# Moving the splitting of squares and keys from ScalarE and VectorE to GpSimd in the second attention, with the norm one unit later

## The chip, the cores and the metric

The kernel runs on one core of a Trainium2 chip. The metric is the device time of one execution in microseconds (us), as the median of several runs. A core has five engines with instruction queues of their own: TensorE (PE, matmuls; PEld its weight loads), VectorE (DVE), ScalarE (ACT), GpSimd (POOL) and SyncE (SP, which here only issues transfers). Each engine works its list in order and waits on semaphores for the others.

## The reference

Three blocks follow one another on 1024 tokens of width 1024, all in float32: a layer with sliding-window attention and pooling, a layer with a long convolution, and a second block with 16 meta tokens in front (1040 tokens), of which this is the part that matters:

```
y_attn = forgetting_attention(q, k, v, log_f)        # 8 heads of 64, causal, softmax with a decay
y_conv = b_gate * causal_depthwise_conv(c_gate * u, conv_w)
y = concat(head_rms_norm(y_attn, 8, g), head_rms_norm(y_conv, 8, g))
h = h + y @ w_out                                    # then norm, a feed-forward of width 4096, norm
```

`head_rms_norm` divides each head's 64 values of a token by the root of the mean of their squares.

## The kernel before

Values are kept transposed: 128 channels (two heads, a "pair") on the partitions and tokens along the row. A float32 product is made from parts: a value is rounded to a "high" part in TensorE's format (fp32r) and the "low" part is value minus high; the product is then made with both. Rounding is a copy with an output of that type, the low part a subtraction.

The second attention is a list of 80 units (`NU`), 20 for each of four pairs (pair 0 to 3), 10 for each head. A unit is one step over 128 keys, or over three short rests of keys together, for one half of 512 queries. A head has 3 units for its first half and 7 for its second, so that of the 20 units of a pair numbers 2, 9, 12 and 19 end a half (`half_end(m)`, m = 0 to 15 over the whole attention). I call unit 13 of a pair "unit 13", and so on; units count from 0.

In each unit n TensorE does in order: the scores of unit n+2, a "max tile" for the next pair where `MAXES` has one (units 8 to 15 and 17 to 24, where 20 to 24 are units 0 to 4 of the next pair; 8 tiles for each of its heads), a "turn" of the finished maxima where `TURNS` has one (unit 16, and unit 5 of the next pair), the values of unit n (line 1654), and the "head product" of a finished half (lines 1667 and 1668: the sum over a head's channels of its squares, high part and low part, into bank 4). ScalarE does the exponential of each unit (line 2318), the squares `SQ` of a half (2326), their high part `SH` (2331), the keys' high part `KH` of the next pair (2299, in unit 3), the queries' high part `QH` (2304, in unit 4), and the square root of the sums in unit 6 (2335), for which the function table is changed and changed back. VectorE copies the output of a half to `Q` (3082), makes `SL`, the low part of the squares (3087), `KL` and `QL` (3032, 3036), copies the head product's result to `K` (3095, function `norms`), takes the maxima of each max tile (3046; lines 3049 and 3050 end them), the reciprocals (3101), the scaled heads (3106) and their low part `YL` (3111). `CVL` (3115) is the same for the convolution.

What ties them: a max tile waits until VectorE has taken the tile before it (one bank pair is used by all). The first max tile of a pair (unit 8) waits until `extended(c)` on SyncE has brought six transfers of that pair's `KH`, `QH` and decay rows to `KE` and `QE`. SyncE issues them once the high parts of keys and queries are there. All orders are written out by hand; nothing is scheduled by a planner.

GpSimd brings the weights' high parts (`high(p)`: a transfer, line 964) and makes their low parts (`low(p)`, line 973). When the attention starts it also writes the zeros and ones of `KE`, `QE` and `QM` (`init_extended`, `init_slot`), then issues one more weight load with its low part, and has nothing more until the output product after the attention. TensorE's max tile is line 1585 (with its mask 1588), the scores are 1632, 1633 and 1637, the turn is 1600.

## Time and profile before

| | |
|---|---|
| median of 3 runs | 2019.5 us (2018.78 to 2023.27) |
| the profiled execution's own time | 2022.04 us |
| its span in the profile | 2020.2 us |
| mean granted TensorE clock | 0.988 of full speed |
| PE busy / DVE / ACT / POOL, share of the span | 96% / 64% / 36% / 56% |
| the second attention, first scores to first output product | 1105.78 to 1277.84 us of the span |

Times in the rows are us from the start of the span. In a row of the timeline the first number is the start, the second the duration, and the bracket at its end says how long the engine sat idle before it and who ended that. The granted clock is a share of full speed: 1.00 is 2.4 GHz, and 0.50 would be 1.2 GHz throughout.

### The profile page before, as it was taken

The page shows a single profiled execution, that of the slowest core. Times are in us where ns is not written, and L with a number is a line of the kernel's source. Part 1 is how long each engine was busy: PE and PEld are TensorE (multiplying, and loading weights), DVE is VectorE, ACT ScalarE, POOL GpSimd, SP SyncE. Part 2 cuts the span into 40 slices and gives each one's busy share as a digit, 9 for nine tenths or more (in the row PEclk, how much of TensorE's full clock was granted, in tenths as well). Part 3 has the DMA queues.
Part 4 walks back from the last instruction along what each step waited for, and adds up shares of the span by engine and source line. Part 5 has one row for each costly group of instructions (what it writes and reads, how often), then busy time and mean ns, then how long its engine had stood idle before and what let it go on. Part 6 is the DMA issues. An engine that isn't in the chain of part 4 may idle for free.

```text
span 2020.2 us, 25037 instructions
## 1 busy us (share of the span) xinstructions
PE 1946.2 (96%) x9228; PEld 1563.9 (77%) x9228; DVE 1298.9 (64%) x1856; ACT 729.1 (36%) x1221; POOL 1135.9 (56%) x936
## 2 busy tenths in 40 slices
PE   8999999999999999999999989999999999999997
PEld 7787877788777788778887555687788887888886
DVE  5127663679998997251764676467544447777778
ACT  4002653342246443230211554324322324545542
POOL 3221115469989995535442100127777778888884
PEclk8999999999999999999999999999999999999998
DMA  5432117556555554538425442345656768675652
GB/s 193 143 120 72 43 43 250 171 177 188 177 167 176 171 174 148 186 133 257 152 85 133 106 90 53 146 152 161 219 198 224 234 200 299 220 267 206 213 193 99
DMA packets 104504, 335.43 MB, mean 166 GB/s; under 512 B 12672, under 2 KB 12928, under 8 KB 103616
## 3 DMA queue, kind: packets, MB, share of 16 engines
q1 hardware_dynamic: 55616, 192.74, 29.7%
q0 software_dynamic: 30384, 106.44, 15.5%
q10 hardware_dynamic: 18384, 34.66, 4.7%
q8 instruction: 74, 1.21, 0.2%
q14 instruction: 46, 0.38, 0.1%
HBM read 272.75 MB, written 46.20 MB: 158 GB/s over the span
## 4 chain that ended last, share of the span: by engine, by line
issue 33%; POOL 31%; PE 30%; DVE 3%; DMA 2%; ACT 1%; POOLq 0%; SPq 0%; DVEq 0%; ACTq 0%
PE PS L1256 15%; PE PS L1789 13%; POOL WL L973 12%; POOL VSL L1192 3%; POOL RBM L1036 3%; POOL WL L1187 2%; POOL SQH L1036 2%; POOL WH L964 2%; DMA WH<-weights 1%; POOL VS L1184 1%; POOL VS L1179 1%; POOL VS L1176 1%; POOL WL L1194 1%; POOL WH L1162 1%; DVE ACC L3330 1%
## 5 line engine op out<-in xcount | busy, mean ns | idle before, releaser
L1256 PE MATMUL PS<-XHM,WH 128*128 128x512 f32 (+2 forms) x1464 | 525.3, 381 | 18.3 <-POOL WL L973 7.9
L1256 PE MATMUL PS<-XLM,WH 128*128 128x512 f32 (+2 forms) x1464 | 513.0, 373 | 0.0
L1256 PE MATMUL PS<-XHM,WL 128*128 128x512 f32 (+2 forms) x1464 | 512.4, 372 | 0.0
L964 POOL DMA_DIRECT2D WH<-weights x149 | 84.7, 568 | 694.9 <-PE PS L1256 680.0
L973 POOL TENSOR_TENSOR WL<-WRAW,WH 128x1024 fp32r<-128x1024 f32 x149 | 361.1, 2424 | 28.8 <-DMA WH<-weights 20.3
L1256 PEld LDWEIGHTS PS<-XHM,WH 128*128 128x128 f32 x1464 | 270.7, 189 | 80.0 <-issue 15.7
L1256 PEld LDWEIGHTS PS<-XLM,WH 128*128 128x128 f32 x1464 | 277.0, 189 | 49.2 <-issue 1.7
L1256 PEld LDWEIGHTS PS<-XHM,WL 128*128 128x128 f32 x1464 | 276.8, 189 | 48.3
L2770 DVE SCALAR_TENSOR_TENSOR PS<-G,TAPW,PS 128x512 f32<-128x512 f32 x319 | 215.6, 746 | 0.6
L3330 DVE TENSOR_TENSOR ACC<-ACC,PS 128x1024 f32<-128x1024 f32 (+1 forms) x113 | 119.8, 1073 | 16.1 <-PE PS L1256 13.2
L1256 PE MATMUL PS<-OPH,VSH 128*128 128x512 f32 x256 | 99.9, 390 | 2.9 <-issue 2.7
L1256 PE MATMUL PS<-OPH,VSL 128*128 128x512 f32 x256 | 99.6, 389 | 0.0
L1256 PE MATMUL PS<-OPL,VSH 128*128 128x512 f32 x256 | 99.6, 389 | 0.0
L3310 DVE TENSOR_TENSOR OPL<-PS,OPH 128x512 fp32r<-128x512 f32 x98 | 67.5, 689 | 45.6 <-ACT PS L2458 44.5
L2062 ACT ACTIVATE YG<-G,TAPW 128x512 f32<-128x512 f32 x120 | 80.4, 717 | 38.1 <-POOL RBM L1036 31.1
L1654 PE MATMUL PS<-PT,VX 128*128 128x512 f32 (+4 forms) x224 | 85.7, 485 | 6.8 <-ACT PT L2318 6.8
L1192 POOL TENSOR_TENSOR VSL<-VS,VSH 128x512 fp32r<-128x512 f32 x64 | 83.3, 1322 | 5.1 <-ACT VSH L2465 5.1
L2535 DVE TENSOR_TENSOR PS<-PS,SQH 128x512 f32<-128x512 f32 x60 | 41.5, 694 | 61.6 <-ACT SQH L1926 61.1
L1256 PE MATMUL PS<-OPH,WH 128*128 128x512 f32 x192 | 74.9, 390 | 2.3 <-DVE OPL L3306 1.7
L2458 ACT COPY PS<-OPR 128x512 f32<-128x512 f32 x98 | 57.4, 585 | 53.7 <-DVE OPL L3310 53.7
L1036 POOL TENSOR_TENSOR RBM<-RBM,YG 128x512 f32<-128x512 f32 x58 | 74.8, 1290 | 2.8 <-ACT YG L2062 2.8
L2465 ACT ACTIVATE VSH<-VS 128x512 fp32r<-128x512 f32 x64 | 40.1, 632 | 98.1 <-POOL VS L1179 57.9
(383 smaller groups left out, 3979.9 us busy)
## 6 DMA issues: line engine op xcount, KB each, us to landing
WRAW<-weights SPq DMA_DIRECT2D x211, 512.0 KB, 3.5
WH<-weights POOLq DMA_DIRECT2D x195, 512.0 KB, 4.5
OPR<-inner SPq DMA_DIRECT2D x56, 512.0 KB, 6.4
inner<-STAGE ACTq DMA_DIRECT2D x56, 256.0 KB, 4.1
inner<-TOUT ACTq DMA_DIRECT2D x48, 256.0 KB, 4.3
XTOK<-x SPq DMA_DIRECT2D x8, 512.0 KB, 9.6
x_kept<-X SPq DMA_DIRECT2D x4, 1024.0 KB, 8.2
X<-x_kept SPq DMA_DIRECT2D x8, 512.0 KB, 5.5
```

Of the source, the lines that this page charges most:

```text
L964: g.dma_start(WH[:, u, :], weights[WORDER[p]]).then_inc(w_hi[u], 16)
L973: g.tensor_tensor(WL[:, u, :], WRAW[:, u, :], WH[:, u, :].bitcast(F32), ALU.subtract)\
L1036: g.tensor_tensor(tap_acc(q), tap_acc(q), tap_buffer(h, i, q), ALU.add).then_inc(tap_sum[q], 1)
L1192: g.tensor_tensor(VSL[e][:, two], VS[e][:, two], VSH[e][:, two].bitcast(F32), ALU.subtract).then_inc(w_ready, 1)
L1256: m = nc.tensor.matmul(dst[:, a:b], w, v[:, a:b], start=first and n == 0, stop=last and n == 2)
L1654: m = nc.tensor.matmul(o[:, q0 - half * HALF:q0 - half * HALF + w], VX[0:keys, j, c, HD * e:HD * e + P], PT2[n % 3][0:keys, a:a + w], star ...
L1789: m = nc.tensor.matmul(dst, a[:, c], b[:, k, :], start=new and k == 0 and i == 0, stop=k == 3 and i == 2, skip_group_check=True)
L2062: nc.scalar.activation(tap_buffer(h, i, q), col, ACT.Copy, scale=tap).then_inc(tap_product, 1)
L2458: nc.scalar.copy(bank(LOW_BANK), OPR[x][:, a, :]).then_inc(a_hi, 1)
L2770: ins = v.scalar_tensor_tensor(out=src if last else bank(b), in0=src, scalar=weight, in1=bank(was), op0=ALU.mult, op1=ALU.add)
L3310: v.tensor_tensor(OPL[x][:, a, :], bank(LOW_BANK), OPH[x][:, a, :].bitcast(F32), ALU.subtract).then_inc(a_split, 1)
L3330: v.tensor_tensor(dst, dst, src, ALU.add).then_inc(evacuated, 1)
```

## The change

GpSimd takes over 15 of 16 pairs of `SH` and `SL` (`squares_split(m)`; the last stays on ScalarE and VectorE) and the three `KH` of pairs 1 to 3. It does the first `SH`, `SL` and `KH` right behind the constants of `KE` and `QE`, ahead of its last weight load, and the others behind that. TensorE's head product comes 3 units after the end of a half instead of 2, and VectorE's copy of its result (`norms`) 4 instead of 3. Semaphores are renamed and counted apart for keys and queries (`k_hi`; `q2_taken`, which also counts four earlier steps). ScalarE's `queries_hi` now waits itself for the transfers that read the old parts.

```diff
@@ SyncE, extended(c)
-                sp.wait_ge(kq_hi, 2 * c + 2)
+                sp.wait_ge(k_hi, c + 1)
+                sp.wait_ge(q2_taken, 4 + c + 1)
@@ GpSimd
+            def keys_hi(c):
+                pool.wait_ge(ext_in[(c - 1) % 2], 96 * ((c - 1) // 2 + 1))
+                for e in range(2):
+                    pool.wait_ge(slot_in[e], 80 * c)
+                g.tensor_copy(KH2[:], K2[:, c, :]).then_inc(k_hi, 1)
+
+            def squares_split(m):
+                pool.wait_ge(o2_sq, m + 1)
+                g.tensor_copy(SH2[m % 2][:], SQ2[m % 2][:]).then_inc(o2_hi, 1)
+                pool.wait_ge(o2_hi, m + 1)
+                g.tensor_tensor(SL2[m % 2][:], SQ2[m % 2][:], SH2[m % 2][:].bitcast(F32), ALU.subtract).then_inc(o2_lo, 1)
+
                     init_extended(1)
                     initialized(4)
+                    squares_split(0)
+                    keys_hi(1)
+                if p == P_OUT2 + 2:
+                    for m in range(1, 2 * HEADS - 1):
+                        if m % 4 == 0 and m // 4 + 1 < PAIRS:
+                            keys_hi(m // 4 + 1)
+                        squares_split(m)
@@ TensorE
-                    if n - 2 in ended:
-                        head_norm(ended[n - 2])
+                    if n - 3 in ended:
+                        head_norm(ended[n - 3])
@@ ScalarE
-                if n - 1 in ended:
-                    squares_hi(ended[n - 1])
                 c, s = divmod(n, 2 * PER_HEAD)
-                if s == 3 and c + 1 < PAIRS:
-                    keys_hi(c + 1)
@@ VectorE
                 if n in ended:
                     output2(ended[n])
-                if n - 1 in ended:
-                    squares_lo(ended[n - 1])
-                if n - 2 in ended:
-                    norms(ended[n - 2])
+                if n - 3 in ended:
+                    norms(ended[n - 3])
```

GpSimd's list at the start of the attention, from the last constant (`SMALL` is only a mark) on. Before:

```order
L1026 MEMSET SMALL 128x1
L964 DMA WH<-weights 128x1024
L973 TENSOR_TENSOR WL<-WRAW,WH 128x1024
L964 DMA WH<-weights 128x1024
L973 TENSOR_TENSOR WL<-WRAW,WH 128x1024
```

and with the change:

```order
L1027 MEMSET SMALL 128x1
L1109 CAST SH_0_125<-SQ_0_118 128x512
L1111 TENSOR_TENSOR SL_0_123<-SQ_0_118,SH_0_125 128x512
L1105 CAST KH_99<-K_89 128x1040
L965 DMA WH<-weights 128x1024
L974 TENSOR_TENSOR WL<-WRAW,WH 128x1024
L1109 CAST SH_1_126<-SQ_1_119 128x512
L1111 TENSOR_TENSOR SL_1_124<-SQ_1_119,SH_1_126 128x512
```

The weight load and its subtraction, the first thing behind the constants before, stand behind two roundings and a subtraction.

VectorE's list in units 10 to 14 of pair 1. Before:

```order
L3082 COPY Q_91<-PS 64x512
L3101 RECIPROCAL K_89<-K_89 128x256
L3046 TENSOR_REDUCE SMALL<-PS 128x1
L3087 TENSOR_TENSOR SL_1_124<-SQ_1_119,SH_1_126 128x512
L3106 SCALAR_TENSOR_TENSOR Q_91<-Q_91,GAINS,K_89 128x1024
L3046 TENSOR_REDUCE SMALL<-PS 128x1
L3095 COPY K_89<-PS 64x512
L3046 TENSOR_REDUCE SMALL<-PS 128x1
L3082 COPY Q_91<-PS 64x512
L3111 TENSOR_TENSOR YL<-Q_91,YH 128x1024
L3046 TENSOR_REDUCE SMALL<-PS 128x1
```

and with the change:

```order
L3094 COPY Q_91<-PS 64x512
L3113 RECIPROCAL K_89<-K_89 128x256
L3058 TENSOR_REDUCE SMALL<-PS 128x1
L3118 SCALAR_TENSOR_TENSOR Q_91<-Q_91,GAINS,K_89 128x1024
L3058 TENSOR_REDUCE SMALL<-PS 128x1 x2
L3094 COPY Q_91<-PS 64x512
L3107 COPY K_89<-PS 64x512
L3123 TENSOR_TENSOR YL<-Q_91,YH 128x1024
L3058 TENSOR_REDUCE SMALL<-PS 128x1 x3
```

`SL` is gone, and the copy to `K` has moved from ahead of the maxima of unit 12 to between the copy to `Q` and `YL` of unit 13.

## Rows read from the trace of the kernel before

**Rows 1.** The page, its first line.
```profile
span 2020.2 us, 25037 instructions
```

**Rows 2.** Windows: the attention; busy us and (instructions) by engine, clock, DMA share, GB/s.
```profile
1105.78:1277.84 172.06, 153.05 (x709) 96.14 (x710) 113.83 (x152) 85.83 (x143) 10.64 (x13) 0.98 0.37 81
```

**Rows 3.** Timeline of PE: stops, first max tile, one turn.
```profile
1118.30 0.71 PE L1667 MATMUL PS<-SH,HN 128*128 128x512 f32 x1 [1.86 <-DVE SL L3087]
...
1125.61 0.31 PE L1585 MATMUL PS<-KE,QE 128*128 128x144 f32 x1
...
1160.27 0.27 PE L1600 MATMUL PS<-IDENT,SMALL 128*8 128x128 f32 x1
...
1165.65 1.56 PE L1654 MATMUL PS<-PT,VX 128*128 128x512 f32 x2 [2.05 <-ACT PT L2318]
...
1175.37 0.50 PE L1585 MATMUL PS<-KE,QE 128*128 128x512 f32 x1 [0.80 <-DVE SMALL L3046]
...
1183.07 0.68 PE L1585 MATMUL PS<-KE,QE 128*128 128x512 f32 x2 [1.41 <-DVE SMALL L3046]
...
1188.03 0.27 PE L1600 MATMUL PS<-IDENT,SMALL 128*8 128x128 f32 x1 [0.36 <-DVE SMALL L3050]
...
1263.17 0.50 PE L1667 MATMUL PS<-SH,HN 128*128 128x512 f32 x1 [0.56 <-DVE SL L3087]
...
1269.10 0.50 PE L1667 MATMUL PS<-SH,HN 128*128 128x512 f32 x1 [0.67 <-DVE SL L3087]
```

**Rows 4.** Windows: behind the first stop; pair 1 and pair 2, unit 7 to unit 11.
```profile
1118.30:1122.12 3.82, 3.82 (x8) 2.17 (x9) 3.74 (x4) 2.82 (x4) 0.00 (x0) 0.55 0.99 213
...
1165.65:1175.37 9.72, 8.92 (x38) 5.58 (x38) 6.70 (x9) 3.38 (x7) 0.00 (x0) 0.82 0.65 138
1211.39:1219.52 8.13, 7.33 (x37) 4.61 (x37) 6.70 (x9) 3.38 (x7) 0.00 (x0) 1.00 0.78 163
```

**Rows 5.** GpSimd: two roundings' nearest kin, a subtraction of 512, the weights' subtraction.
```profile
L985 POOL CAST IDENTB<-IDENT 128x128 bf16<-128x128 f32 x1 | 0.3, 289 | 0.1
L1010 POOL TENSOR_SCALAR_AFFINE_SELECT QE<-QE 64x1024 fp32r<-64x1024 f32 x4 | 4.1, 1036 | 0.6 <-POOL QE L1009 0.2
L1192 POOL TENSOR_TENSOR VSL<-VS,VSH 128x512 fp32r<-128x512 f32 x64 | 83.3, 1322 | 5.1 <-ACT VSH L2465 5.1
...
1115.32 2.36 POOL L973 TENSOR_TENSOR WL<-WRAW,WH 128x1024 fp32r<-128x1024 f32 x1
```

**Rows 6.** Timeline of VectorE, start of the attention.
```profile
1115.81 2.44 DVE L3087 TENSOR_TENSOR SL<-SQ,SH 128x512 fp32r<-128x512 f32 x1 [1.34 <-ACT SH L2331]
1118.17 1.23 DVE L3032 TENSOR_TENSOR KL<-K,KH 128x1040 fp32r<-128x1040 f32 x1
...
1121.21 3.48 DVE L3115 TENSOR_TENSOR CVL<-G,CVH 128x1024 fp32r<-128x1024 f32 x3
```

**Rows 7.** SyncE's queue, first of the six transfers for pair 1; the window of them.
```profile
1116.82 0.53 SPq L746 DMA_DIRECT2D KE<-KH  x1
...
1116.25:1123.12 6.87, 5.01 (x14) 2.69 (x13) 6.79 (x6) 5.42 (x9) 1.43 (x1) 0.75 0.93 225
```

**Rows 8.** Timeline of VectorE: maxima of unit 4, then units 12 and 13 of pair 1.
```profile
1158.56 1.22 DVE L3046 TENSOR_REDUCE SMALL<-PS 128x1 f32<-128x1024 f32 x1
...
1177.64 0.67 DVE L3095 COPY K<-PS 64x512 f32<-64x512 f32 x1
...
1180.06 0.69 DVE L3082 COPY Q<-PS 64x512 f32<-64x512 f32 x1 [0.76 <-ACT SQ L2326]
1180.78 1.23 DVE L3111 TENSOR_TENSOR YL<-Q,YH 128x1024 fp32r<-128x1024 f32 x1
1182.04 0.97 DVE L3046 TENSOR_REDUCE SMALL<-PS 128x1 f32<-128x784 f32 x1
```

**Rows 9.** ScalarE: the squares, and the roundings that leave it, grouped by form.
```profile
L2326 ACT ACTIVATE SQ<-PS,HSCALE 128x512 f32<-128x512 f32 x16 | 11.0, 687 | 28.8 <-PE PS L1654 28.8
...
L2331 ACT ACTIVATE SH<-SQ 128x512 fp32r<-128x512 f32 x16 | 10.1, 630 | 0.0
```

More of the change, by code:

```diff
@@ L473, in build @@
         ext_init = sem("ext_init")
-        kq_hi = sem("kq_hi")
+        k_hi = sem("k_hi")
         kq_lo = sem("kq_lo")
@@ L498, in build @@
         hn_inv = sem("hn_inv")
-        yc_sq = sem("yc_sq")
+        q2_taken = sem("q2_taken")
         yc_sum = sem("yc_sum")
@@ L1686, in attention2 @@
                     values(n)
-                    if n - 2 in ended:
-                        head_norm(ended[n - 2])
+                    if n - 3 in ended:
+                        head_norm(ended[n - 3])
             def heads_conv(c):
-                pe.wait_ge(yc_sq, c + 1)
+                pe.wait_ge(q2_taken, c + 1)
                 if c >= 1:
@@ L2255, in _ @@
                 wait_freed(act, (IN2, I_B + c, 1))
-                nc.scalar.activation(Q2[:, c, :], CU[:, c, META:], ACT.Square).then_inc(yc_sq, 1)
+                nc.scalar.activation(Q2[:, c, :], CU[:, c, META:], ACT.Square).then_inc(q2_taken, 1)
             def value_taken(n):
@@ L2290, in _, with keys_hi, queries_hi @@
                 value_taken(n)
-            def keys_hi(c):
-                if c >= 1:
+            def keys_hi():
+                wait_freed(act, (IN2, 20, 1))
+                nc.scalar.activation(KH2[:], K2[:, 0, :], ACT.Copy).then_inc(k_hi, 1)
+            def queries_hi(c):
+                if c == 0:
+                    act.wait_ge(evacuated, USE[C_IN2 + I_Q] + 1)
+                else:
                     act.wait_ge(ext_in[(c - 1) % 2], 96 * ((c - 1) // 2 + 1))
@@ L2296, in keys_hi @@
                         act.wait_ge(slot_in[e], 80 * c)
-                else:
-                    wait_freed(act, (IN2, 20, 1))
-                nc.scalar.activation(KH2[:], K2[:, c, :], ACT.Copy).then_inc(kq_hi, 1)
-            def queries_hi(c):
-                if c == 0:
-                    act.wait_ge(evacuated, USE[C_IN2 + I_Q] + 1)
-                nc.scalar.activation(QH2[:], Q2[:, c, :], ACT.Copy).then_inc(kq_hi, 1)
+                nc.scalar.activation(QH2[:], Q2[:, c, :], ACT.Copy).then_inc(q2_taken, 1)
             def max_hi(h):
@@ L2343, in conv_hi @@
                 nc.scalar.activation(CVH[:, c, :], CU[:, c, META:], ACT.Copy).then_inc(cv_hi, 1)
-            keys_hi(0)
+            keys_hi()
             queries_hi(0)
@@ L2372, in _ @@
                     max_hi(TURNS[n])
-            for m in range(2 * HEADS - 1):
-                if half_end(m) + 2 >= NU:
-                    squares_hi(m)
             squares(2 * HEADS - 1)
@@ L3030, in keys_lo @@
             def keys_lo(c):
-                dve.wait_ge(kq_hi, 2 * c + 1)
+                dve.wait_ge(k_hi, c + 1)
                 v.tensor_tensor(KL2[:, c, :], K2[:, c, :], KH2[:].bitcast(F32), ALU.subtract).then_inc(kq_lo, 1)
             def queries_lo(c):
-                dve.wait_ge(kq_hi, 2 * c + 2)
+                dve.wait_ge(q2_taken, 4 + c + 1)
                 v.tensor_tensor(QL2[:, c, :], Q2[:, c, :], QH2[:].bitcast(F32), ALU.subtract).then_inc(kq_lo, 1)
@@ L3143, in _ @@
             output2(2 * HEADS - 1)
+            squares_lo(2 * HEADS - 1)
             for m in range(2 * HEADS):
-                if half_end(m) + 2 >= NU:
-                    squares_lo(m)
-            for m in range(2 * HEADS):
-                if half_end(m) + 3 >= NU:
+                if half_end(m) + 4 >= NU:
                     norms(m)
```

## Prediction, before the changed kernel was run

> **What bounds the kernel now.** I read the page first: a span of 2020.2 us [rows 1], against 2022.04 us for that execution's own time and 2019.5 us for the median, so 1.8 us lie around the span and the profiled execution was 2.5 us slower than the median. I add what I find to the median. The change touches only the second attention. Its window [rows 2] shows PE busy 153 of 172 us, DVE 114, ACT 86, POOL 11. So TensorE bounds the stretch, ScalarE has half its time free, and taking work off it is worth nothing by itself. What can be won is the 19 us in which TensorE stands, plus what a low clock costs. Then I read the timeline of PE for its stops [rows 3]. The reader is to see four kinds:
>
> - 1.86 us on `SL` at the start; then 0.56 and 0.67 us on `SL` in pair 3, where no max tiles fill the time. Sum 3.1 us. These are what the change is made of.
> - 2.05 us behind the square root, when ScalarE changes tables (three times, in unit 7 of pairs 1 to 3).
> - 0.80 and 1.41 us at the max tiles of units 11 and 14, on VectorE's maxima (twice each, pairs 1 and 2).
> - 0.36 us at the turn of unit 16 (three times, pairs 0 to 2), on VectorE again.
>
> The windows [rows 4] add the clock: 0.55 in the 3.82 us behind the first stop, 0.82 behind the 2.05 us stop of pair 1, 1.00 behind the same stop of pair 2. The same work took 9.72 and 8.13 us, so one drop to 1.2 GHz costs 1.6 us.
>
> **Prices on GpSimd.** A rounding of 128x512 isn't in the trace. The cast of 128 elements takes 0.289 us, a one-input operation of 1024 takes 1.036 [rows 5]: 0.83 ns an element and 0.18 fixed, thus 0.61 us for 512 and 1.05 for 1040. The upper bound is a two-input subtraction of that size, 1.32 us (and 2.4 for 1040). I take the lower, since the cast is the same instruction. A split is then 0.61 + 1.32 + 0.15 between them = 2.1 us (at most 2.8) from the squares on. TensorE asks for it three units later, each 172/80 = 2.15 us on average, so in the steady part no head product waits for `SL`. The Trainium skill, "GPSIMD Engine Reference", section 4.1, has one-input work "roughly line-rate"; the two rows agree with that.
>
> **The start of the attention.** Before, `SL` took 2.44 us instead of 0.68 beside the weights' subtraction (1115.32 to 1117.68); it ended 0.57 behind it [rows 5, 6]. A VectorE instruction with two SBUF inputs stands still while GpSimd reads. Now `SL` is on GpSimd itself: GpSimd is free at 1114.7, so `SH` 0.61, `SL` 1.32, `KH` 1.05 and gaps give `SL` at about 1116.8 and `KH` at 1118.0. TensorE, which was done with unit 4 at 1118.30 - 1.86 = 1116.4, finds its `SL` one unit later without a wait. Its way from there to the first max tile was 1125.61 - 1118.30 = 7.3 us, of which 1.6 were the clock. It could be there at 1116.4 + 5.7 = 1122.1, 3.5 us earlier than before. Two things stand in front of that.
>
> First, the six transfers for that max tile. SyncE issued the first at 1116.82 when `QH` was there; now it waits for `KH`, 1118.0. The weight load of 512 KB was issued 2 us ahead of them, and now falls among them, at 1118.0 to 1118.6. At 225 GB/s the window of 6.87 us moved 1.55 MB, which is the load and the six (0.52 + 1.04 MB) [rows 7]. Both together begin now some 1.5 us behind their issue, about 1119.3, and are over at 1126.1 if they share evenly, at 1124.5 if the load ends last. I take 1125.7: the max tile comes when it came before.
>
> Second, VectorE. `KL` began at 1118.17 and begins at 1118.05 now. Behind it come `QL` (1.2), the copy to `K` (0.68) and three `CVL` (3.48) [rows 6, 8], over at 1124.7 before. The weights' subtraction (2.36) now falls on this row of two-input instructions: `QL` or a `CVL` stands still for it, and the row ends at 1127.0. The maxima of unit 8 end at 1127.5, and the second max tile waits 0.5 us or so for them.
>
> So TensorE stands for 3.5 us ahead of unit 8, at the place of the 1.86 us, and with that the clock should fall as it did there, for 1.6 us. **Term: +1.5 us** (bounds: -1.0, transfers by 1124.5 and no drop; +3.0, roundings at the upper bound).
>
> The rule that speaks against this change stands in the Trainium skill, "SBUF — State Buffer", section "Who interferes with whom": a VectorE instruction with two SBUF inputs and a GpSimd instruction that reads SBUF exclude each other for a whole instruction. By that rule, the trace agrees: 2.44 against 0.68 us.
>
> **Units 12 to 14 of pairs 1 and 2.** The stop of 1.41 us is a chain from the end of unit 12's values: squares on ScalarE 0.69 [rows 9], copy to `Q` 0.69, `YL` 1.23, maxima 0.97 [rows 8], max tile. The copy to `K` (0.67) now stands in this chain, between `Q` and `YL`. And GpSimd wakes on the same squares: `SH` for 0.61, then `SL` from 0.9 to 2.2 us behind them, while `YL` wants to start 1.4 us behind them. `YL` stands still till 2.2, 0.8 us. Against that the chain begins 0.6 us earlier: the head product went from unit 11 to behind the values of unit 12 (two matmuls of 512 columns at 2.4 GHz, 0.21 us each, some 0.47 with the gaps), and the removed `SL` (0.67) lets VectorE follow. -0.6 + 0.67 + 0.8 = +0.9; gaps between queues are less in the longer chain, I take **+0.6 each, +1.2**. Bounds: -0.4 in all if `YL` gets in first (with a rounding of 1.3 us it does), +1.8 if the subtraction is slower beside it.
>
> **The turn of unit 16**, three times 0.36 us: the head product now stands between the last max tile and the turn, and fills that stop. **-1.1.** The 0.80 us stop of unit 11 hangs on the squares, the copy to `Q` and a reciprocal, of which none moves: 0.
>
> **Units 2 to 5.** The copy to `K` also comes into the chain from the end of unit 2 through squares, `Q` and the maxima of unit 3 to the max tile of unit 4, which TensorE meets without a stop today, I take it just so: 0.67 less the 0.47 us of the moved head product is 0.2, three times, and the same once in unit 13 of pair 0: **+0.8**. The turn in unit 5 follows the maxima of unit 4: they end at 1159.78, the two small closing operations follow, the turn is at 1160.27 [rows 3, 8]. So the chain VectorE, turn, ScalarE, table change, values is what gives the 2.05 us stop its end. Moving the head product from ahead of the turn to behind it shortens the stop and not the time: 0.
>
> **Pair 3.** 0.56 + 0.67 = **-1.2**, as `SL` is there. `YL` may be late behind GpSimd, but no max tile waits.
>
> **ScalarE** loses 15 x 0.63 us [rows 9] and three roundings of keys. It waits for TensorE most of the time, so 0.
>
> Sum: +1.5 + 1.2 - 1.1 + 0.8 - 1.2 = **+1.2 us**, 2020.7 us. What 3 runs of this kernel can tell from no change is about 0.2%, 4 us. So I forecast no measurable change.
>
> **The rivals.**
>
> *The start is won (faster).* If the transfers land by 1122 and the weights' subtraction meets VectorE's copy from PSUM rather than `QL` and `CVL`, TensorE runs through: -3.5 with the clock kept, and `YL` in front of GpSimd (-0.4). -3.5 - 0.4 - 1.1 + 0.8 - 1.2 = -5.4, 2014.1 us. For it: the 1.86 us stop and its clock drop are real, and `SL` no longer suffers. Against it: 1.55 MB at 225 GB/s, started 1.2 us later, can't be there by 1122. Chance 0.2.
>
> *The clock falls more often (slower).* The new stops of 2.2 us at unit 14 (1.41 and 0.6 more, with 0.2 of the moved head product) are as long as the one that cost 1.6 us in pair 1. If both, and one more of the three behind the square root, are followed by 1.2 GHz: 3 x 1.6 = 4.8, +6.0 in all, 2025.5 us. It decides from two more drops on (+4.4). For it: a drop behind 1.86, and one of three behind 2.05. Against it: two of three had none. Chance 0.2.
>
> *The change does what it says, and it is worth only that.* If neither GpSimd nor the copy to `K` costs anything, and the start stays tied to its transfers: 0 - 1.1 - 1.2 = -2.3, 2017.2 us. This lies within 0.2% as well and shares the 0.6 with the forecast (0.2 of it).
>
> **How the numbers follow.** Forecast 0.4, the third rival 0.2, the two others 0.2 each. Faster by over 0.2% (under 2015.5): 0.2; slower (over 2023.5): 0.2; within: 0.6. The bounds of the terms, taken together, are -1.0 - 0.4 - 1.1 + 0.8 - 1.2 = -2.9, and -1.6 more if the drop in pair 1 doesn't come, and +3.0 + 1.8 - 1.1 + 0.8 - 0.6 = +3.9 without more drops. The range 2015.0 to 2025.0 takes them in, and leaves out the faster rival's figure and the far end of the slower one.
>
> **What would show it.** Right: no stop on `SL` anywhere but at the last half; a stop of 3 us or more ahead of the first max tile of pair 1, ended by a transfer, and a low clock behind it; one of VectorE's two-input instructions near 1119 to 1125 lasting over 3 us; `YL` of pairs 1 and 2 lasting 2 us; the stop of unit 14 at about 2 us; no stop at unit 16; the rounding of 512 near 0.6 us. Wrong: the first max tile at 1122 to 1124, `YL` at 1.23 us, or roundings of 1.3 us and more, with `SL` late for its head product.

## The result, and the profile after

The changed kernel takes 2024.57 us (median of 22 runs, 2020.53 to 2034.54), the kernel before 2019.57 us beside it (22 runs, 2013.6 to 2024.89). The ratio is 1.0027, 95% interval 1.0019 to 1.0035: slower by 5.0 to 5.5 us. I had forecast 2020.7 us and no change that can be told. The profiled execution took 2026.82 us, with a span of 2025.0; the first line of the page, to be held against [rows 1]:

```profile
span 2025.0 us, 25042 instructions
```

The windows of the attention (columns as in [rows 2]): the whole of it, its start up to the first max tile of pair 1, from there to the turn of unit 16, and the stretch from the turn of unit 5 to that of unit 16 in pair 1 and in pair 2.

```profile
1106.94:1282.41 175.47, 152.78 (x710) 96.89 (x710) 107.66 (x137) 75.47 (x125) 42.00 (x46) 0.97 0.37 79
1106.94:1128.60 21.66, 14.17 (x64) 8.92 (x65) 12.70 (x12) 12.44 (x19) 13.49 (x16) 0.95 0.78 181
1128.60:1147.13 18.53, 18.24 (x78) 11.96 (x79) 9.80 (x16) 4.43 (x8) 3.77 (x4) 0.88 0.20 46
1165.50:1193.22 27.72, 23.39 (x102) 14.16 (x102) 20.85 (x25) 11.76 (x18) 3.78 (x4) 0.94 0.32 69
1211.59:1237.69 26.10, 21.74 (x103) 13.57 (x104) 20.85 (x25) 11.76 (x18) 3.78 (x4) 1.00 0.35 73
```

And the two windows of the kernel before that answer to the second and the third of them:

```profile
1105.78:1125.61 19.83, 16.13 (x64) 9.51 (x65) 12.38 (x13) 13.70 (x20) 10.64 (x13) 0.91 0.74 176
1125.61:1142.25 16.64, 16.13 (x80) 10.49 (x80) 11.67 (x18) 5.99 (x11) 0.00 (x0) 1.00 0.38 78
```

The reader is to see: the attention is 3.41 us longer (175.47 for 172.06). The start alone is 1.83 us longer, and the stretch behind it 1.89, in which TensorE runs the same matmuls (but for one head product) at a clock of 0.88 for 1.00. Of pairs 1 and 2 the same list takes 27.72 and 26.10 us, once with a stretch of low clock and once without: 1.62 us for a stretch, as in [rows 4]. In pair 1 the stretch has moved. Before, it lay behind the stop at the square root [rows 4]; now the clock is 1.00 from there to the max tile of unit 14, and the 3.3 us at 1.2 GHz lie right behind that tile's stop:

```profile
1170.89:1187.09 16.20, 13.45 (x65) 8.65 (x65) 13.22 (x15) 6.74 (x12) 3.78 (x4) 1.00 0.37 78
1187.09:1193.22 6.13, 6.13 (x18) 3.08 (x18) 2.68 (x5) 0.00 (x0) 0.00 (x0) 0.72 0.00 0
```

The stops of TensorE (timeline of PE, to be held against [rows 3]):

```profile
1128.60 0.49 PE L1605 MATMUL PS<-KE,QE 128*128 128x144 f32 x1 [6.06 <-DMA KE<-cum_rows]
...
1162.98 0.73 PE L1605 MATMUL PS<-KE,QE 128*128 128x512 f32 x2 [0.47 <-DVE SMALL L3058]
1165.50 0.27 PE L1620 MATMUL PS<-IDENT,SMALL 128*8 128x128 f32 x1 [0.27 <-DVE SMALL L3062]
1170.89 1.12 PE L1674 MATMUL PS<-PT,VX 128*128 128x512 f32 x2 [1.58 <-ACT PT L2337]
...
1187.09 0.68 PE L1605 MATMUL PS<-KE,QE 128*128 128x512 f32 x2 [1.96 <-DVE SMALL L3058]
```

No stop on `SL` is left in the attention, and none at the turn of unit 16. In their place stand 6.06 us ahead of the first max tile, on a transfer; 0.47 us at the max tile of unit 4; and 1.96 us at unit 14, where it was 1.41.

VectorE and GpSimd at the start (timelines; [rows 6] and the last of [rows 5] before), and SyncE's first and last transfer for the max tile ([rows 7]):

```profile
1116.24 1.28 POOL L1111 TENSOR_TENSOR SL<-SQ,SH 128x512 fp32r<-128x512 f32 x1
...
1117.48 1.04 POOL L1105 CAST KH<-K 128x1040 fp32r<-128x1040 f32 x1
...
1118.47 0.57 POOL L965 DMA_DIRECT2D WH<-weights  x1
...
1118.56 4.00 DVE L3044 TENSOR_TENSOR KL<-K,KH 128x1040 fp32r<-128x1040 f32 x1 [2.93 <-POOL KH L1105]
...
1118.68 0.54 SPq L747 DMA_DIRECT2D KE<-KH  x1
...
1119.07 2.38 POOL L974 TENSOR_TENSOR WL<-WRAW,WH 128x1024 fp32r<-128x1024 f32 x1
...
1122.54 0.59 SPq L749 DMA_DIRECT2D KE<-cum_rows  x1
```

`KL` takes 4.00 us for 1.23: the weights' subtraction has the memory from 1119.07 to 1121.45, and `KL` ends 1.1 us behind it at 1122.56. `KH` ends at 1118.52 and the first transfer is issued 0.16 us later, 11.74 us behind the first scores for 11.04 before.

Unit 13 of pair 1, timeline of VectorE and GpSimd ([rows 8] before):

```profile
1183.07 0.69 DVE L3094 COPY Q<-PS 64x512 f32<-64x512 f32 x1 [0.77 <-ACT SQ L2345]
...
1183.10 0.61 POOL L1109 CAST SH<-SQ 128x512 fp32r<-128x512 f32 x1 [4.95 <-ACT SQ L2345]
...
1183.79 0.68 DVE L3107 COPY K<-PS 64x512 f32<-64x512 f32 x1
...
1183.79 1.28 POOL L1111 TENSOR_TENSOR SL<-SQ,SH 128x512 fp32r<-128x512 f32 x1
...
1184.40 1.75 DVE L3123 TENSOR_TENSOR YL<-Q,YH 128x1024 fp32r<-128x1024 f32 x1
```

and GpSimd's groups by form, whose mean in ns is the number ahead of the last bar:

```profile
L1105 POOL CAST KH<-K 128x1040 fp32r<-128x1040 f32 x3 | 3.1, 1048 | 2.2 <-DMA QM<-QL 2.2
L1109 POOL CAST SH<-SQ 128x512 fp32r<-128x512 f32 x15 | 9.2, 610 | 120.7 <-ACT SQ L2345 120.6
L1111 POOL TENSOR_TENSOR SL<-SQ,SH 128x512 fp32r<-128x512 f32 x15 | 19.2, 1277 | 1.2
```

`YL` takes 1.75 us for 1.23 and ends at 1186.15, 1.1 us behind GpSimd's `SL` (1185.07).

### The profile page after: what moved, and what is told of

The parts are those of the page before. It is cut to its first block, busy times and chain, and to the rows that moved or that the text cites. A ratio compares the mean times of both kernels' runs of the same rounds, so it can differ in the third digit from the quotient of the medians.

```text
span 2025.0 us, 25042 instructions
## 1 busy us (share of the span) xinstructions
PE 1948.0 (96%) x9228; PEld 1565.6 (77%) x9228; DVE 1292.4 (64%) x1841; ACT 718.6 (35%) x1203; POOL 1166.8 (58%) x969
## 3 DMA queue, kind: packets, MB, share of 16 engines
q8 instruction: 74, 1.21, 0.2%
## 4 chain that ended last, share of the span: by engine, by line
PE 34%; POOL 31%; issue 27%; DVE 4%; DMA 2%; ACT 2%; SPq 0%; POOLq 0%; DVEq 0%; ACTq 0%
PE PS L1276 15%; PE PS L1809 13%; POOL WL L974 13%; POOL VSL L1212 3%; POOL RBM L1037 3%; PE PS L1674 2%; POOL WL L1207 2%; POOL SQH L1037 2%; POOL WH L965 2%; DMA WH<-weights 1%; POOL VS L1204 1%; POOL VS L1199 1%; PE PS L1605 1%; POOL VS L1196 1%; POOL WL L1214 1%
## 5 line engine op out<-in xcount | busy, mean ns | idle before, releaser
L3318 DVE TENSOR_TENSOR OPL<-PS,OPH 128x512 fp32r<-128x512 f32 x98 | 67.6, 690 | 45.4 <-ACT PS L2470 44.5
L2082 ACT ACTIVATE YG<-G,TAPW 128x512 f32<-128x512 f32 x120 | 80.4, 717 | 38.1 <-POOL RBM L1037 31.2
L1109 POOL CAST SH<-SQ 128x512 fp32r<-128x512 f32 x15 | 9.2, 610 | 120.7 <-ACT SQ L2345 120.6
```

What stands on the lines that cost most here:

```text
L2082: nc.scalar.activation(tap_buffer(h, i, q), col, ACT.Copy, scale=tap).then_inc(tap_product, 1)
L3318: v.tensor_tensor(OPL[x][:, a, :], bank(LOW_BANK), OPH[x][:, a, :].bitcast(F32), ALU.subtract).then_inc(a_split, 1)
```

## How the experiments are read

The table gives every kernel that ran. "To tile" is the time from the first scores to the first max tile of pair 1, "to turn" from there to the turn of unit 16 of pair 0, "att." the whole attention, all in us, from one profiled execution each. "Low" is the time at 1.2 GHz in the attention, worked out as 2 x (1 - granted clock) x length, summed over its eight sections between turns. The ratio is of timed runs against the kernel before.

| kernel | to tile | to turn | att. | low | median | ratio (95% interval) |
|---|---|---|---|---|---|---|
| before | 19.83 | 16.64 | 172.06 | 6.9 | 2019.57 | |
| before, second look | 21.26 | 16.64 | 171.91 | 6.8 | | |
| after | 21.66 | 18.53 | 175.47 | 9.9 | 2024.57 | 1.0027 (1.0019 to 1.0035) |
| after, second look | 21.38 | 18.66 | 175.25 | 9.9 | | |
| e1_defer | 19.22 | 21.12 | 182.06 | 27.6 | 2025.87 | 1.0021 (1.0009 to 1.0034) |
| e2_keys | 20.34 | 22.30 | 184.35 | 31.2 | 2023.84 | 1.0025 (1.0009 to 1.0041) |
| e6_hold | 21.66 | 18.42 | 175.31 | 10.3 | 2025.74 | 1.0022 (1.0009 to 1.0034) |
| e8_kcopy | 21.76 | 17.85 | 174.85 | 16.8 | 2022.11 | 1.0011 (1.0000 to 1.0021) |
| e10_ylfirst | 21.82 | 21.05 | 177.96 | 17.1 | 2022.72 | 1.0016 (1.0004 to 1.0028) |
| e5_sooner | 21.55 | 18.79 | 175.40 | 10.0 | 2022.81 | 1.0023 (1.0011 to 1.0034) |
| e4_later | 19.94 | 16.32 | 172.08 | 6.9 | 2017.93 | 0.9984 (0.9971 to 0.9996) |
| e9_best | 19.98 | 17.28 | 172.49 | 6.9 | 2019.39 | 0.9994 (0.9983 to 1.0005) |
| e12_fill | 21.45 | 16.31 | 171.38 | 0 | 2017.51 | 0.9984 (0.9971 to 0.9997) |
| e15_fill8 | 21.53 | 16.31 | 171.62 | 0 | 2023.41 | 1.0009 (0.9998 to 1.0021) |
| e16_fill14 | 21.58 | 18.47 | 173.68 | 6.6 | 2019.40 | 1.0001 (0.9985 to 1.0018) |
| e13_fillb | 18.35 | 16.62 | 172.06 | 6.8 | 2018.74 | 0.9990 (0.9980 to 0.9999) |
| e14_laterfill | 18.48 | 16.32 | 169.07 | 0 | 2019.45 | 0.9996 (0.9985 to 1.0006) |

One caution holds for all of it. Outside the attention these kernels run the same instructions, and yet the first scores stand at 1100.0 us in one profile and at 1108.0 in another, and what follows the attention takes 740.5 to 746.1 us. A single profile says where time goes in the attention, to a few tenths; it doesn't say within 3 us what the median will be.

## Experiments on the start

**e1_defer** does the second `SH` and `SL` ahead of the last weight load, so that this and its subtraction come later.

```diff
                     squares_split(0)
                     keys_hi(1)
+                    squares_split(1)
...
-                    for m in range(1, 2 * HEADS - 1):
+                    for m in range(2, 2 * HEADS - 1):
```

> The changed kernel with its last weight load and that load's subtraction moved on GpSimd from behind the first split and the keys to behind the second split, 13 us later. Theory 1 (the loss is made at the start: late transfers for the first max tile of pair 1, the weight load among them, and the low clock behind the stop): KL takes 1.24 us instead of 4.00, the stop ahead of the first max tile falls from 6.06 us to 3 or 4, the attention (first scores to first output product) from 175.5 us to 172 to 173.5. Theory 2 (the loss is made in units 3 and 13, by the copy to K in the chain and by YL standing behind GpSimd): the stop may shrink, but the attention stays at 175 to 176 us and the time at 1.002 to 1.003 of before.

The max tile comes 2.4 us sooner (19.22) and `KL` runs alone (timeline of VectorE):

```profile
1117.79 1.24 DVE L3045 TENSOR_TENSOR KL<-K,KH 128x1040 fp32r<-128x1040 f32 x1 [2.94 <-POOL KH L1105]
1118.95 1.22 DVE L3049 TENSOR_TENSOR QL<-Q,QH 128x1024 fp32r<-128x1024 f32 x1
```

So the weight load holds the transfers up and its subtraction holds `KL` up. But nothing was won, neither in the timed runs (1.0021) nor in the attention, which both theories had put at 176 us or less and which took 182.06: the windows behind the max tile and of pair 1 show the clock at 0.76 and 0.88, 10.1 and 7.0 us of low clock (and 7.0 again in pair 2).

```profile
1125.38:1146.50 21.12, 20.83 (x79) 13.47 (x79) 9.80 (x16) 4.47 (x8) 6.66 (x6) 0.76 0.33 76
1164.87:1194.21 29.34, 24.99 (x102) 15.15 (x102) 21.00 (x25) 11.75 (x18) 3.78 (x4) 0.88 0.31 65
```

**e6_hold** has SyncE issue the next transfers (those of pair 1's scores) only when the six have landed.

```diff
             for c in range(1, PAIRS):
+                if c == 1:
+                    sp.wait_ge(ext_in[1], 96)
                 slots(2 * c)
```

> The changed kernel with one wait more on SyncE: the five transfers of slots(2) are issued only when the six for the first max tile of pair 1 have landed. In the changed kernel they were issued 1.2 us behind the last of the six, since TensorE had been early. Theory 1a (they share the bandwidth with the last of the six): the stop falls from 6.06 us to about 3.9, the first max tile comes 2.2 us earlier, the attention is 173 to 173.5 us. Theory 1b (the six are slow by themselves, with the weight load): the stop stays at 6 us.

The stop is 6.06 us again. The traffic that follows the six costs them nothing. This kernel also shows what my forecast of the landing left out, since nothing else runs behind the six. Windows of 1 us, first transfer issued at 1112.84, max tile released at 1122.75:

```profile
1113.09:1114.09 1.00, 1.00 (x6) 0.51 (x4) 1.00 (x1) 1.00 (x3) 0.98 (x2) 1.00 0.34 41
...
1115.09:1116.09 1.00, 1.00 (x5) 0.52 (x5) 1.00 (x1) 1.00 (x3) 0.52 (x1) 1.00 1.09 291
...
1120.09:1121.09 1.00, 0.00 (x0) 0.00 (x0) 1.00 (x2) 0.00 (x0) 0.00 (x0) 0.61 0.64 132
1121.09:1122.09 1.00, 0.00 (x0) 0.00 (x0) 0.76 (x1) 0.00 (x0) 0.00 (x0) 0.50 0.09 25
```

The last two columns are the DMA share and GB/s. The bulk of the bytes flows from about 1113.7 to about 1120.8; the windows add up to some 1.6 MB, which in that time are some 225 GB/s, as I had reckoned. But the flow doesn't end at its full rate. Windows of a quarter of a microsecond:

```profile
1120.00:1120.25 0.25, 0.00 (x0) 0.00 (x0) 0.25 (x1) 0.00 (x0) 0.00 (x0) 1.00 1.04 214
1120.25:1120.50 0.25, 0.00 (x0) 0.00 (x0) 0.25 (x1) 0.00 (x0) 0.00 (x0) 0.63 0.75 148
...
1120.75:1121.00 0.25, 0.00 (x0) 0.00 (x0) 0.25 (x1) 0.00 (x0) 0.00 (x0) 0.50 0.38 82
...
1121.50:1121.75 0.25, 0.00 (x0) 0.00 (x0) 0.25 (x1) 0.00 (x0) 0.00 (x0) 0.50 0.05 16
1121.75:1122.00 0.25, 0.00 (x0) 0.00 (x0) 0.10 (x1) 0.00 (x0) 0.00 (x0) 0.50 0.00 0
```

From 1120.25 on the rate falls, the last bytes come before 1121.75, and TensorE is released at 1122.75. So it is released some 2 us behind the end that bytes and rate would give: about 1 us in which the flow thins out, and 1.0 us between the last bytes and the release. The column ahead of the last two says when the clock fell: between 1120.25 and 1120.50, while TensorE (0.00 busy) had been standing for some 3.6 us.

**e2_keys** leaves the key rounding of pair 1 on ScalarE, in unit 3 as before; GpSimd does only the squares there.

```diff
                     squares_split(0)
-                    keys_hi(1)
...
+                if n == 3:
+                    keys_hi(1)
```

> The changed kernel with the high part of the keys of pair 1 alone back on ScalarE in unit 3, as before the change; the splits and the two other roundings of keys stay on GpSimd. Theory 1: the six transfers begin 1 us or more earlier, the stop ahead of the first max tile is 3 to 4.5 us instead of 6.06, the attention 172.5 to 174 us. Theory 2: 175 to 176 us.

The stop is 4.11 us and the max tile at 20.34, 1.3 us sooner; the clock is low for 12.9 us behind it, and the attention is far longer than either theory said (184.35 us). The time is that of the changed kernel. The key rounding's place is worth 1.3 us of the 3.1 us by which the tile is late, and the weight load 2.4; they overlap.

## Experiments on units 12 to 14 and on the later norm

**e10_ylfirst** lets GpSimd wait with `SL` until `YL` is written, for the halves that meet.

```diff
                 pool.wait_ge(o2_hi, m + 1)
+                if m % 4 == 2 and m >= 4:
+                    pool.wait_ge(y2_split, m // 4)
                 g.tensor_tensor(SL2[m % 2][:], SQ2[m % 2][:], SH2[m % 2][:].bitcast(F32), ALU.subtract).then_inc(o2_lo, 1)
```

> The changed kernel with one wait more on GpSimd: in pairs 1 to 3 the subtraction SL of the half that ends in unit 12 comes behind YL. Theory (YL stands behind that subtraction): YL takes 1.23 us instead of 1.75, the stop of unit 14 falls from 1.96 to 1.45 us, nothing else moves, attention 1.0 us shorter at the same clock. Rival (YL is slow for another cause): 1.75 us again.

Timelines of VectorE and GpSimd in pair 1 of this kernel:

```profile
1183.36 1.21 DVE L3125 TENSOR_TENSOR YL<-Q,YH 128x1024 fp32r<-128x1024 f32 x1
...
1184.71 1.26 POOL L1113 TENSOR_TENSOR SL<-SQ,SH 128x512 fp32r<-128x512 f32 x1 [2.04 <-DVE YL L3125]
```

`YL` takes 1.21 us for 1.75, and the stop of unit 14 is 1.41 for 1.96: GpSimd's `SL` was 0.55 us of that stop. The section from the turn of unit 5 to that of unit 16 gets 0.55 us shorter (25.55 us for 26.10). The attention as a whole didn't get 1.0 us shorter, as forecast for an equal clock, but 2.5 longer (177.96 us): 17.1 us of low clock for 9.9, of which 10.1 lie behind the first max tile (0.76 in 21.05 us), where this edit changes nothing. `SL` also comes late now for a head product of pair 3, a stop of 0.60 us.

**e8_kcopy** puts VectorE's copy to `K` behind the maxima of its unit.

```diff
-                if n - 3 in ended:
-                    norms(ended[n - 3])
...
                 if n in MAXES:
                     max_part(*MAXES[n])
+                if n - 3 in ended:
+                    norms(ended[n - 3])
```

> The changed kernel with VectorE's copy to K put behind the maxima of its unit instead of ahead of them (and so behind YL in unit 13). The copy's 0.67 us leave the chain to the max tile of unit 14 and of unit 4: the stop of 1.96 us falls to 1.3 to 1.6 (YL then begins 0.7 us sooner and meets GpSimd's subtraction for longer, it lasts 2.3 us or gets in first), the stops of 0.47 us in unit 4 go, with a clean clock one pair takes 44.0 us instead of 44.5. If fewer drops of the clock follow the shorter stop, the time is at 1.000 to 1.002 of before; if the start alone decides, 1.002 to 1.003.

The stop of unit 14 falls to 0.93 us, that of unit 4 is gone, and the section from the turn of unit 16 to that of unit 5 takes 17.70 us for 18.37. The copy to `K` in the two chains costs 1.0 us at unit 14 and 0.67 at unit 4, a pair. Ratio 1.0011; the gain of some 4 us in all that these make is partly eaten, as the attention has 16.8 us of low clock for 9.9.

**e4_later** is the kernel before with the head product and the copy to `K` one unit later, and nothing else.

```diff
-                    if n - 2 in ended:
-                        head_norm(ended[n - 2])
+                    if n - 3 in ended:
+                        head_norm(ended[n - 3])
...
-                if n - 2 in ended:
-                    norms(ended[n - 2])
+                if n - 3 in ended:
+                    norms(ended[n - 3])
```

> The kernel before with only the last part of the change: head product and copy to K one unit later, all roundings and subtractions where they were. Theory 1 (GpSimd's part is what costs): the 1.86 us stop on SL and the low clock behind it go, the first max tile of pair 1 comes some 2 us earlier, the stops of 0.56 and 0.67 us in pair 3 go, YL takes 1.23 us: attention 168 to 170.5 us against 172.1, time 0.998 to 0.999 of before. Theory 2 (the later norm costs, by the copy to K in units 3 and 13): attention 172 us or more, time 1.000 to 1.002.

**e5_sooner** is the other half, the changed kernel with `n - 3` put back to `n - 2` in both places.

> The changed kernel with the head product and the copy to K where they were before (two and three units behind the end of a half), the splits on GpSimd. The head product of a half then asks for SL one unit sooner. If GpSimd's splits alone cost the time and the later norm is the part that wins: the first stop on SL is short (SL at 11.6 us behind the first scores, about when TensorE comes for it), the max tile of unit 8 still at 21.6 us, no copy to K in the chain of unit 14 (stop there 1.2 to 1.6 us in place of 1.96), turn of unit 16 with a stop of 0.3 again; ratio 1.002 to 1.005. If the copy to K in that chain is the cost: attention shorter than 175.5 by 1 us or more, ratio about 1.000.

The two halves give 0.9984 and 1.0023. What loses is GpSimd's part of the change: in e5 TensorE stands for 5.06 us ahead of the first max tile, which comes at 21.55 us. In e5 the stops of units 14 and 16 are those of before (1.41 and 0.36 us), and still the attention takes 175.40 us: the cost isn't in that chain. The later norm costs nothing: by its profile it leaves the attention as long as it was (172.08), and the interval of its ratio ends just under 1. The attention of 168 to 170.5 us that I had expected of e4 didn't come. The stop on `SL` is gone, but a stop of 1.61 us on the transfers stands ahead of the first max tile, and there are two stretches of low clock again, the first now some 3 us behind the first scores (clock 0.51 and 0.50 from 1102.97 to 1104.97).

**e9_best** is e4_later with the copy to `K` behind the maxima, and the last weight load behind the second squares.

```diff
                     initialized(4)
+                    pool.wait_ge(o2_sq, 2)
```

> The kernel before with the later head product and the copy to K behind the maxima, and with the last weight load and its subtraction on GpSimd held till the second squares (13 us later); nothing is moved to GpSimd. From what the single parts gave: SL at the start takes 0.68 us, the six transfers have the bandwidth for themselves, the first max tile comes at 17.5 to 19 us from the first scores instead of 19.8, no or a short low clock behind, pairs 1 and 2 take 43.9 to 44.2 us each at full clock, pair 3 0.8 us less. Attention 166 to 169 us, time 0.996 to 0.998 of before.

Its max tile comes at 19.98 us behind a stop of 1.65 on the transfers (e4_later: 19.94 and 1.61), a max tile behind it waits 1.05 us for VectorE, and so does the turn of unit 5, 0.87 us. The expectation (attention 166 to 169 us, ratio 0.996 to 0.998) failed: 172.49 us and 0.9994. Nothing is won over e4_later.

## Experiments on the clock

Here idle matmuls of 512 columns, whose result nobody reads, stand where TensorE would stand still. They are ahead of the wait, and one takes 0.24 us (the 25 of e12_fill 5.94).

**e12_fill**: 25 ahead of the first max tile of pair 1, 7 ahead of the max tile of unit 14 in pairs 1 and 2.

```diff
...
+                if h == 2 and i == 0:
+                    for _ in range(25):
+                        nc.tensor.matmul(bank(6), KE[0][0][:, 0:P], QE[0][0][:, 0:HALF], start=True, stop=True)
                 if i == 0:
                     pe.wait_ge(ext_in[r], 96 * (h // 4 + 1))
```

> The changed kernel with matmuls that compute nothing used, put where TensorE would stand: 25 of 512 columns ahead of the wait for the six transfers (6.06 us before), 7 ahead of the wait of unit 14 in pairs 1 and 2 (1.96 us). They go to banks that are written anew afterwards. No other instruction moves. Theory C (the clock behind the stops makes most of the loss, and its varying length is why single runs differ): the max tiles come at the same places within 0.3 us, no 1.2 GHz behind unit 8, the attention is 171 to 173 us against 175.5, the time at 0.999 to 1.001 of before. Rival (the clock is only a companion, chains of VectorE and transfers set the time behind the stops as well): attention 174.5 us or more, time 1.002 or more.

**e15_fill8** has only the 25, **e16_fill14** only the 7.

> The changed kernel with idle matmuls only in its 6 us stop ahead of the first max tile of pair 1, not ahead of unit 14. If the 6 us stop alone makes the clock fall: clock 1.00 in pair 0, and pairs 1 and 2 without the low stretch that stood there too, attention 172 or less, ratio 0.998 to 0.9995. If the stops of 1.96 us at unit 14 make it fall as well: a stretch of 1.6 us is left in one or two of pairs 1 and 2, attention 173 to 175, ratio 1.000 to 1.002.

> The changed kernel with idle matmuls only ahead of the max tile of unit 14 of pairs 1 and 2, its 6 us stop ahead of the first max tile left as it is. Filled at the start alone it ran at a ratio of 1.0009, filled at both at 0.9984, unfilled at 1.0027. If the two places cost the clock each by itself: ratio 1.0005 to 1.0015, low clock of about 6 us around and behind the first max tile, none in pairs 1 and 2 or one stretch. If the start is the cause and unit 14 only follows: ratio 1.002 to 1.003.

**e13_fillb** is the control: the kernel before, with 7 ahead of its first head product and 5 ahead of the max tile of unit 14. **e14_laterfill** is e4_later with 6 ahead of the first max tile and 5 at unit 14.

> The kernel before, with idle matmuls of 512 columns whose result nobody reads: 7 ahead of the first head product (they fill its stop of 1.86 us) and 5 ahead of the max tile of unit 14 of pairs 1 and 2 (they fill most of 1.41 us). It is the control for the run that filled the stops of the changed kernel. Theory A (low clock behind stops costs the kernel before little, the changed kernel much): the low clock behind the first stop goes, 1.6 us, so the attention takes 170 to 170.5 us, and the ratio to the kernel before is 0.998 to 1.000. Theory B (the filling gains 0.4% in any kernel, whatever the splits do): ratio 0.995 to 0.997 and less scatter of single runs.

> The kernel before with the head product and the copy to K one unit later alone, and idle matmuls in its stops: 6 ahead of the first max tile of pair 1 (stop 1.61 us), 5 ahead of the max tile of unit 14 (1.42 us). If the gain of the later norm and the cost of the clock are separate: the attention at 172.1 less one or two stretches of 1.6 us, 169 to 170.5, ratio 0.996 to 0.998, under both. If the gain of the later norm was only a kept clock, as the filled changed kernel's was, nothing is left to fill and the ratio stays at 0.998 to 0.999.

Windows of the attention of e12_fill, e15_fill8, e16_fill14 and e13_fillb, a row each:

```profile
1101.22:1272.60 171.38, 157.93 (x748) 102.02 (x749) 107.55 (x137) 75.43 (x125) 42.03 (x46) 1.00 0.37 81
```

```profile
1102.59:1274.21 171.62, 154.65 (x735) 99.37 (x735) 107.58 (x137) 75.42 (x125) 42.03 (x46) 1.00 0.37 81
```

```profile
1102.54:1276.22 173.68, 154.26 (x723) 98.88 (x724) 107.10 (x137) 75.42 (x125) 42.63 (x46) 0.98 0.37 80
```

```profile
1103.95:1276.01 172.06, 156.93 (x727) 99.32 (x727) 113.94 (x152) 85.72 (x143) 10.66 (x13) 0.98 0.38 81
```

The reader is to see the column ahead of the last two, the clock. In e12 the first max tile comes when it came in the changed kernel (at 21.45 us), TensorE does more, and the attention is 4.1 us shorter, with the clock at 1.00. In the timed runs that is 0.43% (1.0027 to 0.9984). Each place alone gives a part: 1.0001 with unit 14 filled, 1.0009 with the start filled. The same treatment of the kernel before gives 0.10%. Between the kernels filled in this way, e12 and e13, nothing is left that the timed runs can tell (0.9984 and 0.9990). The idle matmuls make no wait end sooner, so what they give back is the clock's. Several forecasts failed all the same: e13 kept 6.8 us of low clock in the attention (in pairs 1 and 3) and took 172.06 us, not 170 to 170.5; e14 had none and took 169.07 us, as forecast, but its ratio of 0.9996 is under neither theory; and e16's 1.0001 lies below the range of both of its theories.

The mean granted clock of every timed run is also on record, to 0.001. The same formula turns it into time at 1.2 GHz over the whole execution:

| kernel | timed runs | mean clock | low, us | mean span, us |
|---|---|---|---|---|
| before (beside the experiments) | 122 | 0.9887 | 45.4 | 2018.9 |
| after | 22 | 0.9872 | 51.9 | 2023.5 |
| e1_defer | 12 | 0.9867 | 53.6 | 2023.7 |
| e4_later | 12 | 0.9902 | 39.7 | 2016.0 |
| e12_fill | 11 | 0.9910 | 36.3 | 2016.2 |
| e15_fill8 | 12 | 0.9882 | 47.8 | 2021.0 |

The means of low time of the changed kernels are good to some 2 us. The 122 runs were not made beside the 22, and the runs that were have no clock on record; this may shift the difference by a microsecond. A stretch of 3.3 us cost 1.6, so I count half of it as lost. This estimate splits the changed kernel's 4.6 us (2023.5 less 2018.9) into 3.2 of clock and 1.4 of waits. It gives e12 4.6 us of clock back, beside 1.9 us more of waits, and it says why e15 is slower than e12 though its profiled attention is as short: it has 11.5 us more of low clock. Its profile shows where that can lie: a granted clock of 0.988 with none of it in the attention is some 48 us at 1.2 GHz outside. So for the timed runs most of the loss is the clock. That it is the clock behind the longer stops is shown only in so far as filling them took it away.

What isn't shown is the share of each stop. The stretch of low clock in pair 1 went away when the start was filled (e15: 26.17 us for 27.72), and also when unit 14 was (e16: 26.09). In e15 the stops of unit 14 were 2.05 us long and the clock was 1.00 behind them; in both looks at the changed kernel it fell behind the one of pair 1.

**Second looks.** The changed kernel and the one before once more, unchanged, for a profile alone.

> A second look at the changed kernel. If the stretches of low clock in the attention belong to the kernel: again 6 to 7 us of low clock around the first max tile of pair 1 and one stretch of 3.3 us in pair 1 or 2, attention 174 to 177 us. If they belong to the execution: any sum from 0 to 20 us of low clock, attention 171.5 to 182; in both cases the same stops on the same releasers to within 0.1 us.

> A second look at the kernel before. If the stretches belong to the kernel: 3.6 us of low clock behind the stop on SL at the start, one stretch of 3.3 us in pair 1, attention 171.5 to 172.5. If they belong to the execution: 3.6 us at the start and none to three stretches elsewhere, attention 170.3 to 175.

Windows from the first scores to the first max tile of pair 1 and on to the turn of unit 16, changed kernel:

```profile
1107.19:1128.57 21.38, 14.17 (x64) 8.91 (x65) 12.70 (x12) 12.43 (x19) 13.49 (x16) 0.96 0.78 182
1128.57:1147.23 18.66, 18.39 (x78) 12.00 (x79) 9.80 (x16) 4.43 (x8) 3.77 (x4) 0.87 0.21 47
```

and the first of the two in the kernel before:

```profile
1102.85:1124.11 21.26, 17.55 (x64) 10.13 (x65) 12.43 (x13) 13.67 (x20) 10.65 (x13) 0.84 0.70 164
```

The changed kernel has the same stretches in the same places in both looks, 175.47 and 175.25 us. The kernel before has 6.9 and 6.8 us of low clock, 172.06 and 171.91 us, but in the second look all of it lies at the start, behind the stop on `SL` (clock 0.84 in the first section), and none in pair 1. So the difference of the attentions, 3.3 to 3.4 us, holds over two looks each; the place of a stretch of low clock doesn't.

## Why the prediction was wrong, step by step

**The start of the attention is the step that failed.** Forecast +1.5 us, with bounds -1.0 and +3.0. Measured from the first scores to the turn of unit 16: 40.19 us for 36.47, and 0.33 of the removed stop at that turn comes on top: +4.05. It was worked out as "the max tile comes when it came before", and 1.6 us for the clock. Both parts were too small, by some 2.4 us together (the last 0.2 are roundings of the forecast, 1125.7 for 1125.61 and +1.5 for +1.6):

- The tile came at +21.66 us, not at +19.9. `KH` was even sooner than I had it (11.6 us behind the first scores, forecast 12.2), and the rate was right (some 225 GB/s in e6_hold). The end that bytes and rate give was right too: 1120.8 in e6_hold is 19.7 us behind its first scores, forecast 19.9. But I put TensorE's release there. It came 2 us later: the flow thins out for about 1 us, and another 1.0 us passes between the last bytes and the release. In the kernel before such a tail is hidden: its bytes were over by 1123.12 [rows 7], and TensorE came for them at 1125.61. Cost +1.7, in which 0.2 us of clock ahead of the tile are contained (21.45 us in e12).
- The low clock behind the stop cost 18.53 - 16.31 = 2.2 us (16.31 is the same stretch in e12 and e15 at a clock of 1.00), not 1.6. Cost +0.6.

There is an error of thinking in it as well. I took the slow kernel before as the yardstick of its own start. At full clock it reaches the tile at 18.35 us (e13_fillb), and the changed kernel at 21.5: the transfers are 3.1 us late against what the old order can do. The row of PE in e13_fillb, where no bracket says that it waited:

```profile
1122.30 0.30 PE L1593 MATMUL PS<-KE,QE 128*128 128x144 f32 x1
```

**The rest of the sum held, term by term within 0.7 us.** Units 12 to 14: forecast +0.6 each; the section from the turn of unit 5 to that of unit 16 is 0.06 us shorter (26.10 for 26.16 at full clock), of which -0.33 is the turn's stop, so +0.27 each, less than half of the term. The stop itself is 1.96 us (forecast 2.0 to 2.2), `YL` 1.75 (forecast 2.0), GpSimd's `SL` 1.28 (1.32), the roundings 0.61 and 1.05 (0.61 and 1.05, to the hundredth). The turn of unit 16: -1.0 for -1.1. Units 2 to 5: 0.36 us in each of three, +1.1 for +0.8; the stop at unit 4 is 0.47 us. The 2.05 us stop shrank to 1.58 and its end didn't move, as foretold. Pair 3: 27.66 to 26.34, -1.3 for -1.2. Without the start, -0.7 us for a forecast of -0.3. I had also put what can be told from no change at 0.2%; the 22 runs told 0.27% with an interval of 0.08% on each side.

**The lock.** The rule of the Trainium skill, "SBUF — State Buffer", "Who interferes with whom", by which a VectorE instruction with two inputs from SBUF and a reading GpSimd instruction exclude each other, held at both places where I used it (the first time on `KL`, where I had expected `QL` or a `CVL`): `KL` 4.00 for 1.24 us (e1_defer takes the subtraction away from it), `YL` 1.75 for 1.21 (e10_ylfirst). The first cost nothing that can be seen, since the transfers were later still; the second is 0.55 us of each stop of unit 14.

**The rivals.** "The start is won" fell: the transfers didn't come by 1122. "The clock falls more often" forecast 2025.5 us, nearly the measured time, by a mechanism that the profiles don't bear out as put: it wanted drops at both stops of unit 14 and one more at the square root. The stops of unit 14 are there, at 1.96 us, and in pair 1 of both looks the clock fell behind one; but in pair 2 and in e15 it stayed at 1.00, and the drop that the kernel before had behind the square root of pair 1 is gone. In both looks of each kernel there are about two stretches, longer in the changed kernel (9.9 us in all for 6.9). What it had right is that most of the price lies in the clock (3.2 of 4.6 us in the timed runs, by the estimate above) and that filling unit 14 gives time back (1.0027 to 1.0001). That its figure came so near is in part luck.

**What stays open.** At a clock of 1.00 the attention costs 171.38 us changed (e12) against 172.06 less the two stretches of 1.5 and 1.6, about 169.0: +2.4 for the waits and, in the profiles as they are, +1.0 for the clock. The timed median moved by 5.0 to 5.5 us. The profiles thus put most of their 3.4 us on the waits, the timed runs most of theirs on the clock (3.2 of 4.6, by the estimate above). The 2 us that are missing lie outside the attention or in executions that were not profiled; in the profiles the part ahead of it is 1.2 to 4.3 us longer in the changed kernel, with the same instructions, and so it is in some other kernels and not in others. That the filled e12 is as fast in timed runs as e14, though its attention is 2.3 us longer, can't be explained from these profiles either; e14's timed runs had 40.4 us of low clock for e12's 36.3, which is 2 us of time, and why isn't known.

## What to carry to other kernels

When work is moved to an engine whose own queue also starts transfers, follow the transfer to the release of the engine that waits for it: where a profile shows no wait on it, bytes divided by rate give only a lower bound of its landing (here 2 us too early). A stop replaced by a longer one elsewhere can be paid twice, as the stop and as the clock behind it; filling it with idle matmuls tells the two apart in one run, and here gave back 0.43% of the changed kernel and 0.10% of the old one. Where profiles and timed runs disagree, look at the granted clock of the timed runs. Of a change in several parts, time the parts: the norm one unit later alone was 0.16% faster (by the clock, its attention is no shorter, and with its stops filled it was 0.04% faster), the splits on GpSimd alone 0.23% slower.

## What was not expected of the hardware

- The last bytes of the six transfers and the weight load came at a falling rate, 214 GB/s at 1120.0 and 16 at 1121.5, and the matmul that waited for them was released 1.0 us behind the last (e6_hold).
- `KL` is shown as begun 0.5 us ahead of the GpSimd subtraction, and still stood still for the whole of it (1118.56, 4.00 us; subtraction 1119.07 to 1121.45).
- A shorter stop isn't followed by less low clock: with a stop of 3.61 us in place of 6.06, e1_defer's profile had 27.6 us of low clock in the attention for 9.9, and its timed runs as much in all as the changed kernel's (53.6 and 51.9 us). Nor does the stop alone decide: with an untouched start e10_ylfirst had 10.1 us of low clock behind the first max tile for 4.4. A stop of 2.05 us in e15 had none behind it.
